# The recurrent tile of a hybrid decoder trunk as a loop body on the engines, with one copy of its operands and a rotated order of products

## The reference, cut to what matters

```python
def step(state, inp):
    r_t, w_t, k_t, v_t, a_t, b_t = inp
    sa = jnp.einsum('bhij,bhj->bhi', state, a_t)
    state = state * w_t[:, :, None, :] + sa[..., None] * b_t[:, :, None, :] + v_t[..., None] * k_t[:, :, None, :]
    return state, jnp.einsum('bhij,bhj->bhi', state, r_t)
```

## Time and profile before

| | |
|---|---|
| Runs of the kernel before | 4128.37, 4134.59, 4129.63 us; median 4129.63 us |
| The profiled execution: its time, its span | 4129.71 us, 4127.9 us |
| Instructions in the span | 60374 |
| PE busy, weight loads busy | 3684.6 us (89%), 2642.6 us (64%) |
| DVE, ACT, POOL busy | 1853.7 us (45%), 940.7 us (23%), 980.3 us (24%) |
| Mean granted clock of TensorE | 0.91 of full speed |
| First and last start of the level products (L706) | 821.5 and 3065.6 us, in two stretches, one a layer |

### The profile page before, as it was taken

One profiled execution on the slowest core, in us unless ns is written; L12 is line 12 of the kernel. 1 busy time (PEld: TensorE's weight loads), 2 busy tenths in 40 slices (PEclk: granted clock), 3 DMA queues, 4 the chain that ended last, 5 costly groups with the idle time before them and its releaser, 6 DMA issues.

```text
span 4127.9 us, 60374 instructions
## 1 busy us (share of the span) xinstructions
PE 3684.6 (89%) x23288; PEld 2642.6 (64%) x23288; DVE 1853.7 (45%) x3137; ACT 940.7 (23%) x1649; POOL 980.3 (24%) x844
## 2 busy tenths in 40 slices
PE   7888878788899999999988888877888999999997
PEld 3444445577666788888734444456767578888884
DVE  4488887433342222222235888853333512222224
ACT  2121211333212122211121122124332212111222
POOL 1041222144121222222100422232441212222221
PEclk9978886699899999999997888857999999999999
DMA  3000000000010111111110000000001111111110
GB/s 110 34 11 13 14 16 6 16 3 3 27 46 31 51 46 51 46 51 46 36 42 24 16 15 11 16 6 12 4 3 31 51 41 46 51 46 51 46 46 41
DMA packets 38081, 129.42 MB, mean 31 GB/s; under 512 B 7264, under 2 KB 7776, under 8 KB 36960
## 3 DMA queue, kind: packets, MB, share of 16 engines
q1 hardware_dynamic: 37568, 125.29, 9.3%
q10 hardware_dynamic: 288, 1.05, 0.1%
HBM read 120.04 MB, written 5.24 MB: 30 GB/s over the span
## 4 chain that ended last, share of the span: by engine, by line
PE 54%; issue 31%; POOLq 7%; DVE 2%; POOL 2%; ACT 1%; DMA 1%; DVEq 1%; ACTq 0%; SPq 0%
PE bank L957 13%; PE bank L959 13%; PE bank L958 13%; PE bank L706 2%; PE wide L573 2%; PE wide L706 1%; PE wide L578 1%; PE bank L650 1%; PE bank L673 1%; PE wide L636 1%; POOLq L1378 1%; PE bank L847 1%; POOLq L1241 1%; POOLq L1282 1%; PE bank L906 1%
## 5 line engine op out<-in xcount | busy, mean ns | idle before, releaser
L1377 POOL TENSOR_TENSOR WL<-WR,WH 128x1024 fp32r<-128x1024 f32 x160 | 389.9, 2437 | 1494.4 <-ACT WH L1184 1493.7
L603 PE MATMUL bank<-X,WR 128*128 128x512 f32 x1152 | 565.9, 649 | 20.6 <-ACT A L1105 9.5
L957 PE MATMUL bank<-XH,WH 128*128 128x512 f32 x1280 | 517.4, 404 | 19.7 <-DVE XL L1423 10.1
L959 PE MATMUL bank<-XH,WL 128*128 128x512 f32 x1280 | 501.7, 392 | 0.0
L958 PE MATMUL bank<-XL,WH 128*128 128x512 f32 x1280 | 501.5, 392 | 0.0
L603 PEld LDWEIGHTS bank<-X,WR 128*128 128x128 f32 x1152 | 236.0, 211 | 324.8 <-issue 294.2
L957 PE MATMUL bank<-HH,WH 128*128 128x512 f32 x1024 | 400.4, 391 | 0.0
L959 PE MATMUL bank<-HH,WL 128*128 128x512 f32 x1024 | 398.6, 389 | 0.0
L958 PE MATMUL bank<-HL,WH 128*128 128x512 f32 x1024 | 398.4, 389 | 0.0
L1761 DVE TENSOR_TENSOR Y<-Y,bank 128x512 f32<-128x512 f32 x256 | 175.9, 687 | 492.0 <-PE bank L959 492.0
L1498 DVE MAX8 M<-WK 128x8 f32<-128x512 f32 (+5 forms) x372 | 332.0, 892 | 22.6
(11 more groups left out here) (263 smaller groups left out, 5275.8 us busy)
## 6 DMA issues: line engine op xcount, KB each, us to landing
WR<-in_w SPq DMA_DIRECT2D x128, 512.0 KB, 3.5
WR<-in_w_in SPq DMA_DIRECT2D x36, 512.0 KB, 3.5
WR<-in_w_out SPq DMA_DIRECT2D x16, 512.0 KB, 3.5
WR<-in_w_gate SPq DMA_DIRECT2D x16, 512.0 KB, 6.2
Y<-in_xT SPq DMA_DIRECT2D x2, 2048.0 KB, 13.5
out_T<-X SPq DMA_DIRECT2D x1, 4096.0 KB, 11.1
UQ<-in_w_uq SPq DMA_DIRECT2D x2, 1024.0 KB, 7.4
PE_IN<-in_pT SPq DMA_DIRECT2D x2, 1024.0 KB, 4.8
```

The source lines that it names most:

```text
L603: mm = e.matmul(BK_[hf], WR[:, i % RING, kt, :], X[:, kt, hs(hf)], start=kt == 0, stop=kt == KT - 1)
L957: e.matmul(BK_[b], WH[:, s, w, :], high[:, kt, q], start=kt == 0, stop=False)
L959: mm = e.matmul(BK_[b], WL[:, s, w, :], high[:, kt, q], start=False, stop=kt == kts - 1)
L1377: e.tensor_tensor(WL[:, s, :, :], WR[:, i % RING, :, :], WH[:, s, :, :].bitcast(F32), ALU.subtract)
```

## The change

- The tiles t = 0 to 6 become the body of a loop on PE, ACT, POOL and DVE (`e.Fori(0, NB - 1)`); tile 7 stands behind it as a copy of its own, without the work for a next tile.
- AR and AM have one copy instead of two. BM has five instead of two, one a level, so POOL makes all five masks without waiting for the matmuls that read them. ACT copies the receptance part of AR to GT and the values of the next tile to VS (`stage_v`), and DVE adds the outputs' products to GT in place.
- POOL makes the first mask and the seed for heads 0 to 3 at once, which needs banks 0 and 1 alone, and then for heads 4 and 5. The tildes of the next tile come behind all five masks.
- In the levels, even and odd heads no longer go in pairs: PE issues X even, TT odd of the level before, X odd, TI even, TT even, TI odd. ACT's copies follow that order.
- `products(T + 1, 0)` moves from behind `solved` to between the two last TT products, `products(T + 1, 1)` from behind `outputs` to behind `solved`. DVE masks both behind the adds into GT.

The diff, cut to its core (in the functions left out only the index `t % 2` of AR and AM and the argument `t` go):

```diff
-        AR = sb("AR", [P, 2, 3, 2, P], loop)
+        AR = sb("AR", [P, 3, 2, P], loop)
...
-        AM = sb("AM", [P, 2, NH, 4, CH], loop)
-        BM = sb("BM", [P, 2, NH, CH], loop)
+        AM = sb("AM", [P, NH, 4, CH], loop)
+        BM = sb("BM", [P, LEVELS, NH, CH], loop)
...
+        VS = sb("VS", [P, 3, P], loop)
...
-            return slice(t * P, (t + 1) * P)
+            return slice(t * P, (t + 1) * P) if isinstance(t, int) else ds(t * P, P)
...
-            def by_token(T, t):
-
-                for bank, use, src in ((6, "tV", BZ[:, BV:BV + 3, tile_columns(t)]), (7, "tB", BH), (4, "tK", KH),
-                                       (5, "tA", AR[:, t % 2, :, 0, :])):
+            def by_token(T):
+
+                for bank, use, src in ((6, "tV", VS), (7, "tB", BH), (4, "tK", KH), (5, "tA", AR[:, :, 0, :])):
                     free(T, bank, use)
-                    if use == "tB":
+                    if use == "tV":
+                        e.wait_ge(v_staged, T + 1)
+                    elif use == "tB":
                         e.wait_ge(tilde_ready, T * N_TILDE + N_TILDE)
                     for p in range(NP):
                         mm = e.transpose(BK_[bank][:, p * P:(p + 1) * P], src[:, p, :], ident)
                     mm.then_inc(rb[bank].full, 1)
 
-            def levels(T, t):
...
+            def heads3(bank, lhs, rhs, g):
+                for j in range(3):
+                    for c in range(2):
+                        mm = e.matmul(BK_[bank][chunk(c), j * CH:(j + 1) * CH], lhs[chunk(c), 2 * j + g, :],
+                                      rhs[chunk(c), 2 * j + g, :], start=True, stop=True)
+                mm.then_inc(rb[bank].full, 1)
+
+            def merge_x(T, g, i):
+
+                if i == 1:
+                    e.wait_ge(masked, T * N_MASKED + 2)
+                    was_read(T, 2 + g, ("aE", "aO")[g])
+                else:
+                    e.wait_ge(masked, T * N_MASKED + i + 1)
+                    was_read(T, 2 + g, ("TE", "TO")[g] + str(i - 1))
+                free(T, g, ("XE", "XO")[g] + str(i))
+                settle(e)
+                heads3(g, BM[:, i - 1, :, :], TI, g)
+
+            def merge_t(T, g, i):
+
+                was_read(T, g, ("XE", "XO")[g] + str(i))
+                if i == 1:
+                    e.wait_ge(seeds_ready, T * 2 + 2)
+                else:
+                    was_read(T, 4 + g, ("UE", "UO")[g] + str(i - 1))
+                free(T, 2 + g, ("TE", "TO")[g] + str(i))
+                settle(e)
+                heads3(2 + g, TT, XS, g)
+
+            def merge_u(T, g, i):
+
+                was_read(T, g, ("XE", "XO")[g] + str(i))
+                free(T, 4 + g, ("UE", "UO")[g] + str(i))
+                settle(e)
+                heads3(4 + g, XS, TT, g)
+
+            def keys_to_values(T):
+
+                was_read(T, 6, "tV")
+                settle(e)
+                for h in range(NH):
+                    for c in range(2):
+                        mm = e.matmul(BK_[6][chunk(c), h * HD:(h + 1) * HD], AM[chunk(c), h, 2, :],
+                                      VTOK[chunk(c), h, :], start=True, stop=True)
+                mm.then_inc(rb[6].full, 1)
 
...
             def chain(T, c):
 
                 was_read(T, 6 + c, f"M{c}")
-                if c:
+                if c == 0:
+                    free(T, 7, "tB")
+                else:
                     was_read(T, 6, "S0")
                 settle(e)
                 for h in range(NH):
...
-            def rwkv_tile(T, t):
-
-                more = t < NB - 1
-                by_token(T, t)
-                levels(T, t)
+            def rwkv_tile(T, more):
+
+                by_token(T)
+                for i in range(1, LEVELS):
+                    merge_x(T, 0, i)
+                    if i == 1:
+                        keys_to_values(T)
+                    else:
+                        merge_u(T, 1, i - 1)
+                    merge_x(T, 1, i)
+                    merge_t(T, 0, i)
+                    merge_u(T, 0, i)
+                    merge_t(T, 1, i)
+                merge_x(T, 0, LEVELS)
+                merge_u(T, 1, LEVELS - 1)
+                merge_x(T, 1, LEVELS)
+                was_read(T, 4, f"UE{LEVELS - 1}")
+                merge_u(T, 0, LEVELS)
+                if more:
+                    products(T + 1, 0)
+                was_read(T, 5, f"UO{LEVELS - 1}")
+                merge_u(T, 1, LEVELS)
                 solved(T, 0)
                 solved(T, 1)
                 if more:
-                    products(T + 1, t + 1, 0)
+                    products(T + 1, 1)
                 transitions(T)
-                outputs(T, t)
-                if more:
-                    products(T + 1, t + 1, 1)
-                if t:
-                    was_read(T - 1, 7, "S1")
+                outputs(T)
                 chain(T, 0)
                 if more:
-                    seed_products(T + 1, t + 1, 0)
+                    seed_products(T + 1, 0)
                 from_state(T, 0)
                 from_state(T, 1)
                 chain(T, 1)
                 if more:
-                    seed_products(T + 1, t + 1, 1)
+                    seed_products(T + 1, 1)
 
...
-                    products(L * NB, 0, g)
-                    seed_products(L * NB, 0, g)
-                for t in range(NB):
-                    rwkv_tile(L * NB + t, t)
+                    products(L * NB, g)
+                    seed_products(L * NB, g)
+                with e.Fori(0, NB - 1) as t:
+                    rwkv_tile(L * NB + t, True)
+                rwkv_tile(L * NB + (NB - 1), False)
 
...
+            def stage_v(t):
+
+                e.activation(VS[:, :, :], BZ[:, BV:BV + 3, tile_columns(t)], ACT.Copy).then_inc(v_staged, 1)
+
...
                 copy(5, "tA", RHS[:, :, 0:HD], heads(5, HD))
-                for i in lv:
-                    if i < LEVELS:
-                        for g in range(2):
-                            copy(2 + g, ("TE", "TO")[g] + str(i), TI[:, g::2, :], heads(2 + g, CH, 3))
-                    for g in range(2):
-                        copy(4 + g, ("UE", "UO")[g] + str(i), TT[:, g::2, :], heads(4 + g, CH, 3))
+                e.activation(GT[:, :, :], AR[:, :, 1, :], ACT.Copy).then_inc(r_copied, 1)
+
+                def to_ti(g, i):
+                    copy(2 + g, ("TE", "TO")[g] + str(i), TI[:, g::2, :], heads(2 + g, CH, 3))
+
+                def to_tt(g, i):
+                    copy(4 + g, ("UE", "UO")[g] + str(i), TT[:, g::2, :], heads(4 + g, CH, 3))
+
+                for i in range(1, LEVELS):
+                    if i > 1:
+                        to_tt(1, i - 1)
+                    to_ti(0, i)
+                    to_tt(0, i)
+                    to_ti(1, i)
                     if i == 1:
                         copy(6, "AkV", RHS[:, :, HD:P], heads(6, HD))
                         if more:
                             e.wait_ge(tilde_ready, T * N_TILDE + N_TILDE)
                             e.wait_ge(decay_used, T + 1)
                             exps(t + 1)
+                to_tt(1, LEVELS - 1)
+                if more:
+                    stage_v(t + 1)
+                to_tt(0, LEVELS)
+                to_tt(1, LEVELS)
...
-            def tilde(T, t, before_bt=None):
+            def tilde(T, t):
...
-                am = AM[:, t % 2, :, 0, :]
-                for g in range(2):
-                    e.wait_ge(rb[g].free, rb[g].read(T, ("hE", "hO")[g]))
-                    e.wait_ge(rb[2 + g].free, rb[2 + g].read(T, ("aE", "aO")[g]))
+                am = AM[:, :, 0, :]
+                for lo, hi, banks in ((0, 4, ((0, "hE"), (1, "hO"))), (4, 6, ((2, "aE"), (3, "aO")))):
+                    for bank, use in banks:
+                        e.wait_ge(rb[bank].free, rb[bank].read(T, use))
                     settle(e)
-                    e.tensor_tensor(BM[:, 1, g::2, :], am[:, g::2, :], spread(level_mask[1], 3), ALU.mult)\
+                    hh = slice(lo, hi)
+                    e.tensor_tensor(BM[:, 0, hh, :], am[:, hh, :], spread(level_mask[1], hi - lo), ALU.mult)\
                      .then_inc(masked, 1)
-                for g in range(2):
-                    e.tensor_tensor(TT[:, g::2, :], am[:, g::2, :], spread(m0u, 3), ALU.mult)
+                    e.tensor_tensor(TT[:, hh, :], am[:, hh, :], spread(m0u, hi - lo), ALU.mult)
                     e.drain()
-                    e.tensor_tensor(TT[:, g::2, :], TT[:, g::2, :], spread(i64, 3), ALU.add)\
+                    e.tensor_tensor(TT[:, hh, :], TT[:, hh, :], spread(i64, hi - lo), ALU.add)\
                      .then_inc(seeds_ready, 1)
-
-                def level(i):
-                    if i > 2:
-                        e.wait_ge(rb[1].full, rb[1].written(T, f"XO{i - 2}"))
-                    e.tensor_tensor(BM[:, i % 2, :, :], am, spread(level_mask[i], NH), ALU.mult).then_inc(masked, 1)
-
```

(57 more changed lines are left out.)

52 lines of the change are left out of this document (22 added, 30 removed).

## The result

The changed kernel takes 4060.5 us (median of four runs, 4055.8 to 4065.5) against 4131.6 for the kernel before, a ratio of 0.9828 with a 95% interval of 0.9811 to 0.9845: 71 us less where 41 were forecast. The profiled execution after is the longest of the four (4065.5 us, span 4063.7); against the span before, 4127.9, it is 64 us shorter. The interval leaves about 7 us either way, so 64 and 71 agree.

The account below looks back on a forecast made before the run. Tiles were taken as a ladder of PE, DVE and ACT steps plus 3.3 us of PE instruction-block stops. Twelve passes at -3.2 us (-38), first pass 0, tile 7 -3: 4129.7 - 41 = 4089 us, range 4070 to 4122.

Parts of the forecast that it names:

- block stops gone: PE in passes 1 to 6: stops for new instruction blocks vanish, 3.3 us a tile, at most 39.6 us in all.
- branch and registers: Loop on the engines: 0.1 us charged for the branch back, 0.1 us for register work at the head, each tile.
- level 1, POOL's early step: Start of a tile: POOL masks two heads before X instead of three; second X at 3.6 us instead of 4.6, -1.0.
- rotated levels, with the exponentials' wait: Levels 2 to 4: 2.33 us each instead of 2.62, -0.9; ACT's four exponentials delay TI odd of level 2, +0.5.
- The body stays: PE keeps the loop's tile body of 5.5 instruction blocks, so later passes fetch nothing and have no block stops.
- The order gives 24.5 against 24.5: Step latencies from P, POOL's last first-level mask, to the next, without stops: no net gain; bounds 1.2 us either way.
- rival 2: The order wins in full, 1.2 us in fourteen tiles more: 4072 us; chance 0.12.
- The tail: GT adds to next tile: state copy waits behind DVE's two masks, PE stands 1.3 us at second from_state; 5.6 us.
- 1: Body does not stay with PE: stops remain, each branch back takes up to 3.4 us; 4166 us; chance 0.13.
- 3: The order loses 1.2 us a tile, by the tail and by ACT's queue: 4106 us; chance 0.13.
- 4: Branch cheap on PE, but ACT, DVE or POOL gets its next block some 3 us late: about 4127 us; chance 0.04.
- 5: Blocks are still fetched, without a stop at the branch: 4126 us; chance 0.04.

Follow-up runs that it names:

- buffers_alone: Changed kernel with tiles written out, levels in pairs, products in old places and POOL's first masks and seeds by even and odd heads: 28.86 us a tile, 4130.9 us.
- loop_alone: Changed kernel, loop kept, with levels in pairs, products in old places and POOL's first masks and seeds by even and odd heads: 25.07 us a tile, 4090.9 us.
- loop_pairs: Changed kernel, loop kept, with levels in pairs again and the next tile's products in their old places: 23.77 us a tile, 4068.2 us.
- loop_prod_back: Changed kernel with only the next tile's products back in their old places, levels in the new order: 22.76 us a tile, 4054.6 us.
- run 4: Changed kernel with two tiles in the loop body, three passes, tiles 6 and 7 behind it: 27.9 us a tile, 4116.9 us.
- best: Changed kernel with state copies on ACT, exponentials behind level 2 and DVE's two MT writes behind the first level's XS: 23.02 us a tile, 4055.8 us.

## Why the prediction was wrong in size

The mechanism was right and two terms of the sum were mis-sized: the loop's gain, forecast at 3.1 us a pass and measured at 3.8, and the new order, put at nothing and measured at 1.0 us a tile. The per-tile sum was 28.2 - 3.3 (stops) + 0.2 (loop), with the order at zero: 25.1, written as 25.0, since the list's gap to the mean went in as 0.3 where it is 28.2 - 27.8 = 0.4. The runs give the terms by differences along one path: buffers_alone - before, loop_alone - buffers_alone, loop_pairs - loop_alone, loop_prod_back - loop_pairs, change - loop_prod_back.

| Term, us a tile | I said | Measured |
|---|---|---|
| block stops gone | -3.3 | -3.8 |
| branch and registers | +0.2 | within the -3.8 |
| level 1, POOL's early step | -1.0 | -1.3 |
| rotated levels, with the exponentials' wait | -0.9 + 0.5 = -0.4 | -1.0 |
| products moved; buffers and DVE's later masks | about +1.4 | +0.6 and +0.7 |
| sum | -3.1 | -4.8 |

- **"The body stays": right.** No packet in twelve passes, and the branch takes 0.21 us.
- **The 3.3 us: mis-sized.** The sum of idle time on "issue" left out stops that end under another engine's name and those shorter than a matmul record. Less the branch they measured 3.8, and 4.3 in the tighter order; that fewer hide behind waits there was not tested. I had also written that the rows allow no more than 39.6 us; that bound was false, since a row's releaser is inferred. The prediction's own list held a sign of it: 28.2 less the 24.5 us of the ladder is 3.7, of which it called 3.3 stops and carried the remainder over as a cost of every tile.
- **"The order gives 24.5 against 24.5": the step that failed most.** The ladder had the right shape, but its first rungs were set 0.2 us late, the others 0.07, and the wait for the exponentials was 0.37 us and not 0.5. From P, with my figures in brackets: second X 3.38 (3.6), fifth X 10.55 (11.1), transitions 15.65 (16.45), GT adds 18.06 (18.9), and 5.26 (5.6) more to the next P at 916.53: 23.3 us for 24.5. By the runs, the rows of POOL's step and of the levels belong together, as my -1.0 for level 1 held a part of both: -2.3 against -1.4. The last row is +1.3 for +1.4. The order was rival 2's, nearly in full (1.0 of its 1.2 us).
- **The tail: right in mechanism.** The state copy behind two masks was the wait I named, and moving the products did not pay. I did not see that DVE has no gap there, so that more than PE's wait would have to go.
- **The first pass, "0": wrong.** It went from 28.75 and 28.76 to 27.44 and 26.05 us, 4 us in all. loop_alone has 28.20 and 27.97 there, so 2.7 us of the four come with the order.
- So 12 x 1.7 = 20 us and 4 us of the 30 missed are explained; the other 6 are about what lies between the profiled execution (64 us less) and the medians (71), which is within the interval.
- **The rivals:** 1 did not come, but run 4 shows it at a larger body; 2 came nearly in full, so 3 did not; against 4 and 5 stands that no packet came in the twelve passes. The range took 3.3 us of stops as the most that the loop could give, so its low end had only the order's 1.2 us in it. The loop gave 0.7 more on top of that, 8 us in twelve passes, and no case held both.

## What to carry to other kernels

Price a stall by the difference of two kernels or of two passes, or by starts against starts, not by adding up the idle rows: part of it hides under other names. Before moving work out of a stretch, ask which engine has no gap there: PE's products taken out of a tail that DVE fills gained nothing and cost 0.6 us where they went. Make a repeated stretch a loop if its body is of a size that stays, and look for the absence of instruction packets to see whether it does.

## What the runs showed of the hardware

- PE keeps a loop body of 5.5 blocks of 16 KB, but not one of 11: then the packets come again (5.7 a tile) and a branch back takes 3.5 us instead of 0.21. The kept body shows no stop but the wait behind ACT's copy (0.9 us in six tiles for 16.3); streamed code loses 3.8 to 4.3 us in 5.5 blocks, though its queue has to bring only one block of 16 KB in about 5 us. The 16 KB of a block are those of q8's packets, 0.54 MB in 33.
- DVE and POOL slow each other: the two MT writes take 0.89 us beside one mask of POOL in the change and 2.04 us beside its four masks in best. That mask of heads 4 and 5 takes POOL 0.62 us in the change and 0.45 us in best, where MT is written later. The Trainium skill, "SBUF — State Buffer", Terms, says that the two share a port pair which the loser waits for in full; these rows agree, and the copies of matmul results stayed at 0.35 us.
